# Gate a's first column block over both halves, pooling sums spread through it, and five smaller moves in a hybrid decoder layer

## What is computed

```python
h = rmsnorm(x) * g_mix
u, q, k, v, og, zr, ga, gb = split(h @ w_in)       # 512, 256, 256, 512, 512, 16, 1024, 1024
# A: 4 groups of 128 channels, trailing windows w = 2, 4, 8, 16
pooled[g] = window_sum(u[g], w) / w - u[g]
y_a = ((pooled[g] @ w_group[g]) * scale) @ w_pool_proj
# B: 4 heads; per-token decay exp(log_sigmoid(zr @ w_gk_up + b_gk) / 16)
att = causal((q e^b) @ (k e^-b)^T);  o = (q e^b) @ S + att @ v;  S = decay * S + (k e^(b_last-b))^T @ v
y_b = (rmsnorm_per_head(o) * g * silu(og)) @ w_gla_proj
x = x + (sigmoid(ga) * y_a + sigmoid(gb) * y_b) @ w_out
h2 = rmsnorm(x) * g_ffn
x = x + (silu(h2 @ w_gate) * (h2 @ w_up)) @ w_ffn_out      # d_model 1024, d_ff 2816
y = rmsnorm(x) * g_final
```

## Time and profile before

| | |
|---|---|
| Median of 3 runs | 903.97 us (903.27 to 904.07) |
| The profiled execution | 904.85 us, span 903.7 us on core 2 |
| Spans of the eight cores | 898.2 to 903.7 us |
| TensorE busy | 876.8 us, 97% of the span |
| VectorE, ScalarE, POOL busy | 430.5, 260.7, 133.3 us |
| Bytes moved by DMA | 100.50 MB, mean 111 GB/s |

### The profile page before, as it was taken

How to read it: one execution, slowest core, us unless ns; L and a number is a source line. 1 busy time by engine, 2 the same in 40 slices (tenths; PEclk the granted TensorE clock), 3 DMA queues, 4 the chain that set the end, 5 groups by cost and what they waited for, 6 DMA issues and landing times.

```text
span 903.7 us, 14522 instructions; the slowest of 8 cores (898.2 to 903.7 us)
## 1 busy us (share of the span) xinstructions
PE 876.8 (97%) x4885; PEld 447.7 (50%) x4885; DVE 430.5 (48%) x715; ACT 260.7 (29%) x515; POOL 133.3 (15%) x249
## 2 busy tenths in 40 slices
PE   5999899999999999999999999999999999999996
PEld 2444566654664566456644444444444444444443
DVE  4684665656435322432367765565651331232146
ACT  4562533223222122012236514332231011101123
POOL 5534112002100000100022001120120000000002
PEclk9999899999999999999999999999999999999999
DMA  8984833849719825953795995454874854362504
GB/s 201 219 155 59 162 51 39 140 75 170 118 43 154 183 39 92 157 100 62 115 164 174 213 202 78 59 85 49 126 112 68 128 94 64 59 112 47 93 24 164
DMA packets 57548, 100.50 MB, mean 111 GB/s; under 512 B 41586, under 2 KB 42226, under 8 KB 50308
## 3 DMA queue, kind: packets, MB, share of 16 engines
q0 software_dynamic: 10768, 66.75, 45.8%
q1 hardware_dynamic: 46564, 32.63, 15.2%
q10 hardware_dynamic: 144, 0.20, 0.1%
HBM read 139.36 MB, written 11.53 MB: 167 GB/s over the span
## 4 chain that ended last, share of the span: by engine, by line
PE 91%; DMA 3%; DVE 2%; issue 2%; ACT 1%; POOL 1%; DVEq 0%; POOLq 0%; ACTq 0%; SPq 0%
PE ps L431 87%; DMA ring<-w_f 1%; DMA R<-R 1%; DVE R L324 1%; PE ps L870 1%; DMA xres<-xm 1%; PE ps L782 1%; ACT R L316 0%; PE ps L763 0%; PE ps L550 0%; PE ps L416 0%; PE ps L783 0%; PE ps L541 0%; POOL stat L320 0%; PE ps L740 0%
## 5 line engine op out<-in xcount | busy, mean ns | idle before, releaser
L431 PE MATMUL ps<-hT,ring 128*128 128x368 bf16 (+2 forms) x2720 | 507.7, 344 | 2.5 <-DMA ring<-w_f 1.6
L431 PEld LDWEIGHTS ps<-hT,ring 128*128 128x128 bf16 x2720 | 261.2, 98 | 230.4 <-issue 8.0
L314 ACT ACTIVATE sgt<-ps 128x368 f32<-128x368 f32 (+2 forms) x207 | 109.7, 531 | 435.1 <-PE ps L431 382.4
L431 PE MATMUL ps<-ring,R 128*128 128x512 bf16 (+2 forms) x1028 | 222.5, 377 | 0.0
L320 DVE TENSOR_TENSOR R<-ps,sgt 128x368 bf16<-128x368 f32 (+1 forms) x110 | 66.1, 601 | 237.6 <-PE ps L431 230.2
L431 PEld LDWEIGHTS ps<-ring,R 128*128 128x128 bf16 (+1 forms) x1028 | 101.2, 99 | 118.4 <-issue 1.2
L320 DVE TENSOR_TENSOR xres<-xres,ps 128x512 f32<-128x512 f32 (+2 forms) x103 | 69.8, 681 | 66.0 <-PE ps L431 65.4
L431 PE MATMUL ps<-R,ring 128*128 128x368 bf16 (+1 forms) x320 | 71.2, 345 | 0.0
L316 ACT ACTIVATE R<-xres 128x1024 bf16<-128x1024 f32 (+3 forms) x45 | 45.8, 1018 | 82.9 <-DVE xres L324 43.4
L187 POOL DMA_DIRECT2D ring<-w_f x34 | 18.7, 550 | 294.7 <-PE ps L431 293.4
L431 PE MATMUL ps<-ring,hT 128*128 128x512 bf16 (+1 forms) x248 | 54.8, 379 | 0.7 <-ACT hT L314 0.7
(11 more groups left out here) (120 smaller groups left out, 457.9 us busy)
## 6 DMA issues: line engine op xcount, KB each, us to landing
ring<-w_f POOLq DMA_DIRECT2D x30, 1024.0 KB, 12.5
ring<-w_a POOLq DMA_DIRECT2D x23, 1024.0 KB, 10.7
y_p<-xres SPq DMA_DIRECT2D x15, 512.0 KB, 2.8
xres<-xp POOLq DMA_DIRECT2D x8, 512.0 KB, 11.7
R<-xp SPq DMA_DIRECT2D x8, 512.0 KB, 11.0
xres<-xp SPq DMA_DIRECT2D x8, 512.0 KB, 29.5
ring<-w_f POOLq DMA_DIRECT2D x4, 768.0 KB, 12.4
R<-sgla SPq DMA_DIRECT2D x2, 1024.0 KB, 9.8
```

What stands on the lines that cost most here:

```text
L314: T.op('act', lambda e: e.activation(out=out, in_=in_, func=func, scale=scale, bias=bias), reads=rd, writes=wr)
L431: return [(lambda e, k=k: e.matmul(out, lhsT=lw(k), rhs=rx(k), start=(k == 0), stop=(k == K - 1))) for k in range(K)]
```

## The change

Six edits. (1) In the head of pass 0, `nb(3)` goes ahead of `n1s(5)`, and `n1s(6)` and `n1s(7)` come after `nb(4)`. (2) The pool products of block A (pass 1: A and B) are taken one group behind each projection of q and k of block B. (3) The keys of units 0 and 1 are transposed by TensorE in `sA1`, in both passes; the transposing DMAs of block A cover units 2 and 3 only. (4) In pass 0 block X is done for both halves of gate a before the pool products of block B and the blocks Y and Z; a step of the pooling sums is taken at every second of the eight steps of the first half and at the first seven of the second. (5) In the output projection the last two units take their first halves together, and slab 10 is released behind them. (6) At the end of pass 1 the last unit's scaling and store go ahead of those of the unit before it.

```diff
@@ -589,7 +589,10 @@
                     tt(keT[:, c, c0:c0 + n], ps, eiT[:, c, :], ALU.mult)
                     if blk != 'S':
                         u0 = c0 // 128
-                        xpose(keTM[:, u0:u0 + 4, c * 128:(c + 1) * 128], keT[:, c, c0:c0 + 512])
+                        if u0 == 0:
+                            xpose(keTM[:, 2:4, c * 128:(c + 1) * 128], keT[:, c, 256:512])
+                        else:
+                            xpose(keTM[:, u0:u0 + 4, c * 128:(c + 1) * 128], keT[:, c, c0:c0 + 512])
                 yield 1.73 * n / 512
 
         def vproj(rg, u):
@@ -742,7 +745,7 @@
                    [keT[:, :, c0:c0 + r], qeZ[:, :, c0:c0 + r]], [ps[:, :]])
                 mk = cs[0:r, C_MAS:C_MAS + SR] if isS else cs[0:r, C_MA:C_MA + 128]
                 tt(am[0:r, :, 0:r], psv[:, :, 0:r], mk.unsqueeze(1).to_broadcast([r, 4, r]), ALU.mult)
-                if isS:
+                if isS or u < 2:
                     bt = nbank()
                     pt = banks_b[bt]
                     pe([(lambda e, c=c: e.transpose(out=pt[0:r, c * 128:(c + 1) * 128], in_=keT[:, c, c0:c0 + r], identity=ident_b[:, :]))
@@ -872,9 +875,8 @@
             for q in range(3):
                 for i in range(3):
                     vq(i, q)
+            nb(3)
             n1s(5)
-            nb(3)
-            n1s(6)
             n1a(4)
             for i in range(3):
                 c0, r, us = ucol(units[i])
@@ -882,8 +884,8 @@
                 cpy(vTM[0:r, us, :], banks[vb[i]][0:r, :])
             for i in range(4, 9):
                 nb(i)
-                if i + 3 < 9:
-                    n1s(i + 3)
+                for k in {4: [6, 7], 5: [8]}.get(i, []):
+                    n1s(k)
                 if i + 1 < 9:
                     n1a(i + 1)
                 vp(i - 1)
@@ -979,18 +981,28 @@
         hold = {}
 
         def dense1():
-            yield from qk(rq, 'B')
+            for g, cost in enumerate(qk(rq, 'B')):
+                yield cost
+                for b_ in (['A'] if has_s else ['A', 'B']):
+                    pool_mix(b_, g)
+                yield 0.22 if has_s else 0.44
             slab_release(j_qk)
-            for b_ in (['A', 'S'] if has_s else ['A', 'B']):
+            if has_s:
                 for g in range(4):
-                    pool_mix(b_, g)
-                yield 0.87 * BLK[b_][1] / 512
+                    pool_mix('S', g)
+                yield 0.2
             j0, r0 = next_slab('a', 4)
             jp, rp = next_slab('a', 5)
             if has_s:
                 late = chain(windows_g('B', 2, glate), windows_g('B', 3, glate))
-                for cost in gate('a', 0, r0, rp, cols[:1]):
-                    next(late, None)
+                for i_, cost in enumerate(gate('a', 0, r0, rp, cols[:1])):
+                    if i_ % 2:
+                        next(late, None)
+                    yield cost
+                j1, r1 = next_slab('a', 6)
+                for i_, cost in enumerate(gate('a', 1, r1, rp, cols[:1])):
+                    if i_ < 7:
+                        next(late, None)
                     yield cost
                 for _ in late:
                     pass
@@ -1003,8 +1015,9 @@
             else:
                 yield from gate('a', 0, r0, rp, cols)
             slab_release(j0)
-            j1, r1 = next_slab('a', 6)
-            yield from gate('a', 1, r1, rp, cols)
+            if not has_s:
+                j1, r1 = next_slab('a', 6)
+            yield from gate('a', 1, r1, rp, cols[1:] if has_s else cols)
             slab_release(j1)
             slab_release(jp)
             hold['jb'], hold['rb'] = next_slab('a', 7)
@@ -1053,17 +1066,26 @@
             ps = tm(rg[:, :], lambda k: w[:, k, :], u, src=merged)
             xh = xres[0:r, us, half * 512:(half + 1) * 512]
             stt(xh, ps, 0.5, xh, ALU.mult, ALU.add)
-        for u in list(range(8)) + (['S'] if has_s else []):
+        ou = list(range(8)) + (['S'] if has_s else [])
+
+        def n2st(u):
             c0, r, us = ucol(u)
-            oproj(u, 0, r0)
-            oproj(u, 1, r1)
             nstat(xres[0:r, us, :], hb_of(u), r, us)
             prev.append(u)
             if len(prev) > 1:
                 v = prev.pop(0)
                 n2a(v)
                 norm_t(hb_of(v), v)
+        for u in ou[:-2]:
+            oproj(u, 0, r0)
+            oproj(u, 1, r1)
+            n2st(u)
+        for u in ou[-2:]:
+            oproj(u, 0, r0)
         slab_release(j0)
+        for u in ou[-2:]:
+            oproj(u, 1, r1)
+            n2st(u)
         slab_release(j1)
         n2a(prev[0])
         norm_t(hb_of(prev[0]), prev[0])
@@ -1251,7 +1273,6 @@
                         final_l(u)
                         down(r1, 1, u, 256, 256)
                         final_q(u, 2, 768, 256)
-                        final(pend.pop(0))
                         pend.append(u)
                         continue
                     down(r1, 1, u)
@@ -1261,7 +1282,8 @@
                         final(pend.pop(0))
                     pend.append(u)
                 if p == 1:
-                    final_w(pend.pop(0))
+                    final_w(pend.pop(1))
+                    final(pend.pop(0))
                 else:
                     final(pend.pop(0))
                 while trq:
```

## The result

The changed kernel takes 919.35 us (median of 4 executions, 916.71 to 1022.55), the kernel before 904.02 us. In some executions of either kernel the cores of one die show a lower clock and take far longer (here the one of 1022.55 us, and one of 964.01 us before); they are left out of every ratio. The ratio is 1.0163, 95% interval 1.0134 to 1.0191: 1.6% slower, 14.7 us. I had forecast 903.1 us in a range of 897.0 to 905.8.

The account below looks back on a forecast made before the run. It took TensorE, busy 876.8 of 903.7 us on core 2, as the bound. Terms summed to 899.7 on core 2 and 902.8 on core 0, the slowest, giving 903.1 us at the median; range 897.0 to 905.8.

Parts of the forecast that it names:

- (1): Head of pass 0: the 0.7 us wait for hT goes, but the chain behind hides it; 0 us.
- (2): Block B of q and k: pool products between projections end waits behind products; -0.7 us, and -0.4 us in pass 1.
- (3): Units 0 and 1 transposed by TensorE: +0.2 us per pass; pass 1's transposing-DMA wait goes, 1.2 us core 2, 0.9 core 0.
- (4): Pooling sums spread: VectorE wait and clock dip go, -5.9 us core 2, -4.5 core 0; four products in a row, +0.4.
- (5): First column block: slab 6 issued late behind POOL's power; wait 2.8 us core 2, 4.7 core 0, plus 1.7 for clock.
- (6): Output projection, pass 1: earlier slab release ends TensorE's slab wait, no new wait; -1.6 us core 2, -1.2 core 0.
- (7): End of pass 1: last unit's scaling goes first, the other tile's store becomes last; +0.5 us, bounds -0.7 and +1.0.
- my slower one, a late slab 6: First column block: slab 6 lands 12.5 us after issue, core 0 waits 6.8 us, time 906.3 us; chance 0.14.

Follow-up runs that it names:

- the slabs held back: Kernel before, with both weight slabs behind the output projection held back in both passes until the last unit's hT has landed: ratio 1.0070.
- TensorE's transposes: Changed kernel, early release kept, hT of units 4 to 7 of pass 1 made by TensorE, not DMA: ratio 1.0227; placed one unit later, 1.0093.

## Why the prediction was wrong

The forecast was 0.9 us down; it was 14.7 us up. By its steps:

(1) Head: 0 forecast, 0 measured (0.9998).

(2) and (3): -1.9 us forecast on core 2, -4.0 measured (interval -2.8 to -5.2). The mechanism is right, the waits at these places are gone. The terms were too small: the wait for the pooling sums shrank as well, from 3.1 to 2.5 us. Where the rest of the gain lies is not shown.

(4) The 3.1 us wait for VectorE is gone, as forecast. The products of block B in a row cost 2.5 us, not 0.4: 1.4 us for ScalarE, as I had it, and 1.1 us for VectorE's products, whose banks TensorE needed back. Edit 4 alone gave 3.1 us, against a forecast of 4.1 (core 0) to 5.5.

(5) The wait for slab 6 behind POOL's power of unit S: issue forecast at 96.6, measured 96.41; wait forecast 2.8 us on core 2 and 4.7 on core 0, measured 4.5 and 3.4. The issue was right; what differed were the landings, 10.5 and 9.4 us after it where I had 8.5 and 10.4. The price of the clock, 1.7 us for both, fell unevenly: in 84 to 120 us core 0 was granted 1.00 behind its 3.4 us of wait, so it paid nothing, core 2 was granted 0.95, cores 1 and 5 0.91. (In the kernel before core 4, too, was granted 1.00 in spite of the same 3.1 us wait as the others.) As a whole the term holds: edits 1, 2 and 3, 4 and 6 measured by themselves add up to about -6 us, together they are at +1.2, so some 7 us are lost only where they meet, against my 4.7 + 1.7. Releasing the slab ahead of that side step gave 3.8 us back, so it was the queue. My estimate by the page of the Trainium skill that I weighed ("DMA: Bandwidth & Descriptors", section "Anatomy of one DMA — SWDGE (gpsimd) path") was 0 to 1.1 us here; the landings of 9.4 to 11.4 us stand against it.

(6) This is the step that failed. I priced the early release of slab 10 at -1.6 us and wrote "no new wait". The wait for the slab did go. But I looked only at who waits for the slab, not at what else the 16 DMA engines carry while it loads. The transposing DMAs of units 5 to 7 now fall beside it and the next one, and take 6.8 to 27.9 us, by core, instead of 3; and SP, held by one issue for up to 13 us, requests the last unit's late. On core 3 block B of the FFN wanted them 17.7 us after unit 6's were issued, so a landing of 13 us would have cost nothing; the landings there cost 11.3 us and the clock. Edit 5 undone (1.0013) shows that it carries 1.5 of the 1.6%; the edit in one pass at a time, that pass 1 pays most of it; its order with the old release, that it is the release; the slabs held back and TensorE's transposes, that the two kinds of DMA delay each other. The trace of before had it: the last unit's transposes, beside the slabs, landed after 13.7 to 17.0 us, its neighbours' after 3. It was hidden there by a demand that comes later. I read the queue of SP only for its order.

(7) Tail: +0.5 us forecast, +1.2 measured (0.3 to 2.1; 1.0 by the end of the span behind the last matmul), the other store last, as forecast.

Without step (6) the change is at 1.0013, 905.1 us on the first chip's scale. My sum with that step at 0 in place of -1.2 on core 0 is 904.3. So the other steps together are right within 1 us, and that is luck in part: the gain of (2) and (3) was put 2.1 us too small, the products in (4) 2.1 us too cheap. None of my rivals was this: my slower one, a late slab 6, had the right sign for another reason.

Of the transposes' delay the trace shows this much more. In 676 to 692 us core 3's DMA engines were busy throughout (a share of 1.26 by the view's count of packet times) and moved 42 GB/s; the slabs nearly alone, in the kernel that holds them back, moved 123 GB/s with less of the engines' time. First the changed kernel, core 3:

```profile
676.00:692.00 16.00, 12.38 (x58) 5.36 (x56) 2.08 (x3) 2.39 (x4) 0.00 (x0) 0.99 1.26 42
```

Then the kernel that holds the slabs back, core 5:

```profile
672.00:684.00 12.00, 8.06 (x38) 3.44 (x36) 2.08 (x3) 1.32 (x3) 1.17 (x2) 0.98 0.71 123
```

The Trainium skill, "DMA: Bandwidth & Descriptors", section "Queues, rings and completion order", says that each DMA engine takes the queues in turn, packet by packet. That fits that each kind is slowed by the other; it does not say why the sum of both runs at a third of the rate, and no run here shows that, nor why an issue then holds SP for 11 to 19 us. Open too is why one core's transposes take 8 us and another's 28 in one execution, and whether the two passes' parts add up by chance or by the slab 6 wait that shifts the cores against each other.

## What to carry to other kernels

Before a load is moved earlier, list every transfer that is under way in the stretch it is moved into, with its time to landing alone and beside such a load, and ask who waits for those. A landing time that is hidden in the trace of before is still a price. Look at how long the issues themselves hold their queue, too: what stands behind one is requested that much later. When a slab's request is in program order behind a small operation of its queue, compute when that operation ends: here this was right to 0.2 us and worth 3.8 us.

## What was not expected of the hardware

A transposing DMA of 128 x 1024 bf16 lands after some 3.1 us alone (at most 5.6 with others of its kind in flight) and after up to 33.0 us beside a 1 MB and a 768 KB weight load with a change of type; its issue occupies the queue of SP for 1.2 to 2.3 us with no such load beside it and for up to 18.8 us there. The 768 KB load, issued some 7 us behind the 1 MB one, takes 8.3 to 31.7 us beside three such transposes, by core, and 7.1 to 9.8 with none. The effect differs between cores of one execution by a factor of three. And a wait of TensorE can be dearer than its length: the kernel that holds the slabs back waits 2.8 to 5.7 us for its slab where the kernel before waits 0 to 1.6, and lost 6.3 us.
